# Two weight tiles instead of three taken chunk by chunk at the entry of the MLP's first matrix

## The reference, cut to what matters

```
u2 = rmsnorm(x, norm_mlp) * (1.0 + scale2) + shift2
h = square(relu(u2 @ w_ff1))          # w_ff1: 1024 x 4096
x = x + gate2 * (h @ w_ff2)           # w_ff2: 4096 x 1024
```

## Time and profile before

| | us |
|---|---|
| median of 3 runs | 996.8 |
| lowest and highest | 988.51, 998.3 |
| the profiled execution, its device time | 985.87 |
| span of its profile, first to last instruction | 984.1 |

### The profile page before, as it was taken

The page is one execution under the profiler, slowest core; times in us unless marked ns, Lnnn a source line. Parts: engine busy times, 40 slices in busy tenths (PEclk is TensorE's granted clock), DMA queues, the critical chain, the costliest instruction groups (busy, mean ns, idle before and its releaser), DMA issues.

```text
span 984.1 us, 21946 instructions
## 1 busy us (share of the span) xinstructions
PE 935.3 (95%) x7758; PEld 910.7 (93%) x7758; DVE 662.6 (67%) x1097; ACT 492.4 (50%) x811; POOL 737.9 (75%) x894
## 2 busy tenths in 40 slices
PE   6899899999889999999999999999998999999996
PEld 6798789999788999999899999999988999999996
DVE  3979996765887676442566678886357666888723
ACT  2455556654345555555444454444454444554441
POOL 1486575687686999897776659999857766799993
PEclk9999999999899999999999999999999999999999
DMA  8985546646453456555444444445524544445531
GB/s 367 392 310 199 199 172 224 225 153 243 159 211 129 174 210 245 210 199 196 152 157 155 167 171 172 171 176 209 182 76 157 177 149 160 172 171 194 189 108 43
DMA packets 28222, 185.20 MB, mean 188 GB/s; under 512 B 3027, under 2 KB 5504, under 8 KB 6272
## 3 DMA queue, kind: packets, MB, share of 16 engines
q1 hardware_dynamic: 25832, 167.93, 47.0%
q10 hardware_dynamic: 2328, 16.40, 4.5%
HBM read 183.26 MB, written 1.07 MB: 187 GB/s over the span
## 4 chain that ended last, share of the span: by engine, by line
PE 72%; DVE 17%; issue 5%; ACT 3%; DMA 1%; DVEq 1%; POOL 0%; SPq 0%; POOLq 0%; ACTq 0%
PE mm L544 21%; PE mm L546 20%; PE mm L545 20%; ACT w_hi L1001 1%; PE mm L578 1%; DVE cy L1967 1%; DVE w_lo L1406 1%; PE mm L562 1%; DVE cy L1972 1%; PE ps_s L871 1%; PE mm L564 1%; PE mm L563 1%; DMA ident<-ident_d 1%; DVE qr L1991 1%; PE ps_o L888 1%
## 5 line engine op out<-in xcount | busy, mean ns | idle before, releaser
L470 POOL TENSOR_TENSOR w_lo<-raw,w_hi 128x256 fp32r<-128x256 f32 x876 | 728.4, 867 | 220.6 <-ACT w_hi L1001 218.0
L544 PE MATMUL mm<-u_hi,w_hi 128*128 128x256 f32 x1608 | 460.2, 286 | 6.2 <-issue 6.0
L545 PE MATMUL mm<-u_lo,w_hi 128*128 128x256 f32 x1608 | 447.2, 278 | 0.0
L546 PE MATMUL mm<-u_hi,w_lo 128*128 128x256 f32 x1608 | 447.1, 278 | 0.0
L1001 ACT ACTIVATE w_hi<-raw 128x1024 fp32r<-128x1024 f32 x291 | 306.4, 1058 | 146.5 <-PE mm L546 141.7
L544 PEld LDWEIGHTS mm<-u_hi,w_hi 128*128 128x128 f32 x1608 | 303.2, 189 | 14.5 <-issue 13.9
L545 PEld LDWEIGHTS mm<-u_lo,w_hi 128*128 128x128 f32 x1608 | 302.5, 188 | 2.0 <-issue 1.9
L546 PEld LDWEIGHTS mm<-u_hi,w_lo 128*128 128x128 f32 x1608 | 302.8, 188 | 0.0
L1406 DVE TENSOR_TENSOR w_lo<-raw,w_hi 128x1024 fp32r<-128x1024 f32 x72 | 102.7, 1426 | 57.8 <-ACT w_hi L1001 55.2
L544 PE MATMUL mm<-mix_hi,w_hi 128*128 128x256 f32 x256 | 71.7, 280 | 1.6 <-DVE mix_lo L1976 1.6
L545 PE MATMUL mm<-mix_lo,w_hi 128*128 128x256 f32 x256 | 71.4, 279 | 0.0
(11 more groups left out here) (292 smaller groups left out, 1342.7 us busy)
## 6 DMA issues: line engine op xcount, KB each, us to landing
raw<-weights SPq DMA_DIRECT2D x145, 1024.0 KB, 4.8
ada_raw<-ada ACTq DMA_DIRECT2D x14, 1024.0 KB, 5.2
ada_raw<-ada SPq DMA_DIRECT2D x6, 1024.0 KB, 12.4
ada_more<-ada SPq DMA_DIRECT2D x4, 1024.0 KB, 12.8
bias<-tab_scratch SPq DMA_DIRECT2D x1, 1536.0 KB, 9.6
dec<-decay ACTq DMA_DIRECT2D x1, 1536.0 KB, 6.6
x<-xT SPq DMA_DIRECT2D x1, 1024.0 KB, 11.1
out<-x SPq DMA_DIRECT2D x4, 256.0 KB, 2.2
```

What stands on the lines that cost most here:

```text
L470: ins = nc.gpsimd.tensor_tensor(w_lo[:, s, at], r[:, at], hi[:, at], ALU.subtract)
L544: nc.tensor.matmul(dst, wh, rhs_hi(k), start=a, stop=False)
L545: nc.tensor.matmul(dst, wh, rhs_lo(k), start=False, stop=False)
L546: i = nc.tensor.matmul(dst, wl, rhs_hi(k), start=False, stop=b)
```

## The change

`first_units` is called for two units instead of three at this place, and the loop over whole units begins at the third. The number of matmuls, loads and splits stays as it was; only PE's order changes, in the 72 matmuls of units 67 to 69.

```
-        first_units(FIRST, U_F1, O_F1, u_ready(1))
+        first_units(2, U_F1, O_F1, u_ready(1))
 
-        for i in range(FIRST, 8):
+        for i in range(2, 8):
             unit(None, U_F1 + i, O_F1 + i, uh, ul)
```

## The result

Over 20 executions each, the changed kernel took 982.97 us in the median (980.65 to 995.28) and the kernel before 989.86 us (983.9 to 999.64). The profiled execution took 982.81 us, its span 980.8.

A forecast was written before the change was run, and what follows sets the result against it. POOL's row was taken to set unit 74; of 2.68 us of waits, 1.20 pay for the entry's gaps and 1.27 are gained. So 996.8 - 1.3 = 995.5 us median (984.6 profiled), range 986.8 to 998.6.

The forecast's parts named there:

- What bounds the stage: MLP entry: POOL's row of twelve instructions, 11.39 us long and begun after ACT's w_hi of unit 72, sets unit 74's start.
- PE's work moves behind the producer: Units 67 to 69: PE waits for each u chunk and finishes unit 69 1.20 us later, a loss.
- Units 67 and 68 end earlier: MLP entry: unit 67's last matmul, ACT's relu_h and POOL's start come 1.27 us sooner, a gain.
- The sum at unit 74: Unit 74 and all behind it move by -1.27 us; POOL stays later than PE by 0.07 to 0.27 us.
- the collision with DVE's w_lo of 75: POOL's row: one quarter takes 1.72 us instead of 0.88; it stays inside the row at the same cost.
- The rule on the shared ports: DVE operations with two SBUF inputs and GpSimd ones reading SBUF fully block each other; one blocked POOL quarter of 1.72 us.
- Rival 1: Granted clock falls between 292 and 303 us, costing PE 1.7 us: +0.4 or +0.3 us overall; chance 0.05.
- How the numbers follow: Whole kernel: -1.3 us at 0.72 gives 984.6 profiled, 995.5 median; execution spread, ends shifted and drawn in, gives 986.8 to 998.6.

The follow-up runs named there:

- a1: Unchanged copy of the changed kernel, run beside the kernel before: median 989.9 us, ratio 1.0006.
- a2: Changed kernel, but ACT's first relu_h waits until unit 69 is done too: median 989.36 us, ratio 0.999 to the kernel before.
- a3: Changed kernel with four weight tiles taken chunk by chunk instead of two: median 991.99 us, ratio 1.0001 to the kernel before.
- d3: Unchanged copy of the changed kernel, in another session: median 985.97 us, ratio 0.996 to the kernel before.
- e0: Changed kernel plus one small matmul between units 74 and 75 and six more keep_warm calls ahead of the last layer's entry: 983.98 us, ratio 0.9928.
- b0: Unchanged copy of the changed kernel: median 984.17 us, ratio 0.9952 to the kernel before.
- d2: Unchanged copy of the kernel before, run against the kernel before: median 991.75 us, ratio 0.9988.
- b1: Kernel before plus seven small matmuls, ahead of the three w_ff1 turns and every eighth w_ff2 unit: median 985.66 us, ratio 0.9957.
- c0: Kernel before plus one small matmul between units 74 and 75 and six more keep_warm calls ahead of the last layer's entry: 985.13 us, ratio 0.9958.
- c3: Changed kernel with c0's additions and four more small matmuls, in each layer's convolution and output projection: median 984.31 us, ratio 0.993 to the kernel before.
- b3: Unchanged copy of the changed kernel, executed once for one more trace: 982.5 us.
- d1: Unchanged copy of the changed kernel: median 987.7 us, ratio 0.9971 to the kernel before.

## Why the prediction was wrong

The way was right, and the mechanism was right in each step that could be read; the size of the measured change and the range weren't.

- *What bounds the stage.* Right. POOL's row behind ACT's first relu_h sets unit 74, shown by a1, a2 and a3: 14.3 to 14.5 us from the one to the other whatever PE's order.
- *PE's work moves behind the producer.* Right: chunks 0.91 apart, unit 69 whole to 2.7 us behind, and no unit waits for it.
- *Units 67 and 68 end earlier.* Forecast 1.27, measured 8.05 - 6.72 = 1.33 against a trace whose entry runs at the slower pace, and 7.77 - 6.72 = 1.05 against one at the quicker.
- *The sum at unit 74.* Forecast -1.27, measured -1.48 or -1.20 in the same two cases. I had 0.07 to 0.27 us of wait left and it is 0.41, because PE came there at 0.1133 a matmul and not at my 0.117 to 0.119; in d3 and e0, whose units 70 to 73 ran at 0.1178, there is next to none of it, and unit 74 starts as early. POOL's row was 0.16 shorter, which I had put at nothing; the collision with DVE's w_lo of 75 stayed inside it, one quarter of 1.72 us, as said.
- *The rule on the shared ports* (the Trainium skill, "SBUF — State Buffer", "Who interferes with whom"): the runs agree at one more place than I used. DVE's first u_lo takes 1.02 or 1.03 us in eleven of the twenty traces, where POOL's last quarter of w_lo of unit 70 ends 0.74 or 0.75 us behind its start, and 0.48 in the other nine, where it ends at most 0.07 behind. That is a draw of 0.55 us which I hadn't seen in the row that I quoted.
- *Rival 1, the clock falls in the entry.* It fell in the MLP's entry in none of the traces (in b0 and e0 it was low for 3.4 us that ended 6 us or more ahead of it), so the rival was rightly given little. But the argument for that was wrong: I took from the earlier trace rows that the last layer's entry keeps the clock. That was one execution. By the mean clocks it fell in half of the others of the same kernel, and in d2's trace, the only one of that kernel's four with such a mean, at exactly that place; a fall costs some 6.5 us.
- *How the numbers follow.* Here the prediction failed, in "All cases lie between -1.6 and +1.2 us" and in a range made of the spread of four executions "drawn in a little". Two steps lay behind it. I treated PE's pace as one number, although 0.119 and 2.81 / 24 = 0.117 stood beside the 0.113 that 1380 matmuls in 156 us give. And I took the spread of 988.5 to 998.3 as noise that a median carries unchanged, with the median of three (996.8) as its centre, where twenty gave 989.86. The range doesn't follow either from its own words: the ends 985.87 and 998.3 less 1.3 are 984.6 and 997.0, and drawn in they give less than 998.6. The runs showed a spread made of a few draws of 6 us each, whose odds a kernel can change. By the pooled means (990.7 of 180 executions, 986.4 of 80) the change is worth 4.3 us. That is pooled over sessions; the ratios of the single sets of the changed kernel lie between 0.994 and 1.0006. Worked out from the counts: 1.2 to 1.5 for the stage, (0.51 - 0.19) x 6.5 = 2.1 for the rarer fall, and (0.56 - 0.32) x 6.0 = 1.4 for the pace, if its odds did change: 4.7 to 5.0. The rest of the first comparison's 6 us is the luck of twenty executions, as are the 0 us of a1.

What stays open is why the odds moved. a2, a3 and b1, whose last-layer entry comes later and not sooner than before, had the fall in 1, 3 and 1 of 12, 12 and 9. That fits with a kernel before whose entry comes at a bad moment for it, rather than with anything the change does well, but it is only argued. What decides which of the two paces PE takes stays open too, and a restart isn't the only place where it changes: in c0's trace it goes from 0.1178 to 0.1133 at 655.5 us, in the middle of a stretch in which no two starts are more than 0.12 us apart.

## What to carry to other kernels

Where several engines hand buffers round, ask which release starts the slowest of them: here it paid to let PE idle for 1.2 us so that one buffer came free 1.3 us sooner, and the price was hidden in waits that existed already. Before a change of a tenth of a per cent is measured, look at what the executions' groups are made of: count matmuls in a stretch where the engine never waits, and list the mean clock of each execution. Removing such draws helped the kernel before by as much as the change does: six calls that fill a pause of 1.4 us, with one small matmul that breaks a long run, took it from 990.93 to 985.13 (ratio 0.9958), and seven such matmuls alone took it from 989.88 to 985.66 (0.9957). In the changed kernel they took the highest executions away, and no gain in its median is shown. The pair with both then differed by 1.7 us, near what the traces say, though twelve and seven executions don't pin it down.

## What the runs showed of the hardware

- fp32r matmuls of 256 columns, back to back and at the full clock, run at 0.1133 or 0.1177 us start to start. Mostly one of them holds from a restart behind a wait to the next interruption, up to 1368 matmuls; in c0 it changed once, at 655.5 us, without one. The busy share is 100% in both. Behind an added small float32 matmul of 128 columns it was 0.1133 in 20 of 22 cases, and in c3, at the same place of two layers, 0.1178 where it is 0.1135 without it.
- PE busy in all 14 us by the profile doesn't bring the clock back up. In a1 each of its turns through the last entry (six matmuls of 256 columns and four of one column) takes longer at the lower level, and the clock stays at 0.50 from 722.1 to 739.2 us; before it fell PE had been busy for 2.62 of 4 us. The same 2.62 of 4 us stand ahead of the entry in b3 and d1, whose clock stays at 1.00, so what PE did there doesn't settle it alone. With the pause of 1.38 us filled, none of 51 executions (c0 to c3, e0) has a mean clock under 0.989. The Trainium skill, "TensorE: Matmul & The Clock Gate", section "A second HAM failure mode: psum-queue depth-cycling", tells of a kernel whose frequent short idle moments between groups of matmuls made the clock alternate. That is not quite this case, with its one pause of 1.38 us. The runs agree in that filling the pause ended the long falls; in the MLP's entry, where PE waits briefly before each chunk, the clock stayed at 1.00 in all twenty traces.
